# Two sets of three PSUM banks for the jobs of the second attention, and a reordered way into it

## The reference

```python
o_a = swa_sink_attention(q_a, k_a, v_a, swa_sinks[l], rel_bias)     # 16 heads of 64, window 128, bias, sink
q_b = jnp.einsum('bsr,rf->bsf', c_q, w_uq[l]).reshape(B, S, MLA_HEADS, MLA_QK_DIM)
q_nope = q_b[..., :MLA_NOPE_DIM]
q_rope = rope(q_b[..., MLA_NOPE_DIM:], positions)
kv_b = jnp.einsum('bsr,rf->bsf', c_kv, w_ukv[l])...                 # keys k_nope and values v_b of 8 heads
# mla: s = (q_nope k_nope + q_rope k_rope) * scale, causal, softmax, times v_b
mix = jnp.concatenate([o_a, o_b], axis=-1)
x = x + g1 * jnp.einsum('bsm,md->bsd', mix, w_out[l])
```

## Time and profile before

| | |
|---|---|
| median of three executions | 2282.96 us |
| span of the profiled execution | 2283.4 us |
| the slowest execution | 2286.44 us |
| TensorE busy | 2212.5 us, 97% of the span |
| VectorE, ScalarE busy | 1511.5 us, 1011.6 us |
| stretch from the query transposes to step 0 of the projection | 1394.08 to 1456.77 us |

### The profile page before, as it was taken

One profiled execution on the slowest core, in us unless ns is written; L12 is line 12 of the kernel. 1 busy time (PEld: TensorE's weight loads), 2 busy tenths in 40 slices (PEclk: granted clock), 3 DMA queues, 4 the chain that ended last, 5 costly groups with the idle time before them and its releaser, 6 DMA issues.

```text
span 2283.4 us, 29520 instructions
## 1 busy us (share of the span) xinstructions
PE 2212.5 (97%) x11498; PEld 1893.8 (83%) x11498; DVE 1511.5 (66%) x1450; ACT 1011.6 (44%) x1261; POOL 15.1 (1%) x40
## 2 busy tenths in 40 slices
PE   7999999999999999999999898999999999999997
PEld 6888888788888888888878697887888888888886
DVE  6676466777777668767788865557555555655655
ACT  5443273544344344344355544535444444443442
POOL 1000000000000000000000000000000000000000
PEclk9999999999999999999999998999999999999999
DMA  8775407687877877878867353355656656556553
GB/s 323 288 277 177 145 23 281 237 279 279 300 258 288 296 269 256 315 258 287 294 238 283 120 193 111 111 192 155 187 193 179 199 194 195 184 186 202 181 196 122
DMA packets 213107, 499.68 MB, mean 219 GB/s; under 512 B 10068, under 2 KB 12680, under 8 KB 199800
## 3 DMA queue, kind: packets, MB, share of 16 engines
q1 hardware_dynamic: 211528, 491.16, 63.3%
q0 software_dynamic: 1456, 6.72, 0.8%
HBM read 495.68 MB, written 2.17 MB: 218 GB/s over the span
## 4 chain that ended last, share of the span: by engine, by line
PE 60%; issue 36%; DVE 2%; ACT 1%; DMA 1%; SPq 0%; POOL 0%; DVEq 0%; ACTq 0%; POOLq 0%
PE ps L1520 17%; PE ps L1509 9%; PE ps L1511 9%; PE ps L1510 9%; PE ps L1525 9%; PE ps L1692 2%; PE ps L1748 1%; PE ps L1567 1%; PE ps L1620 1%; PE ps L1698 0%; PE ps L1584 0%; PE ps L1634 0%; ACT prob L699 0%; PE ps L1749 0%; PE ps L1746 0%
## 5 line engine op out<-in xcount | busy, mean ns | idle before, releaser
L904 DVE TENSOR_TENSOR lower<-raw,upper 128x1024 fp32r<-128x1024 f32 (+2 forms) x733 | 883.7, 1215 | 522.9 <-ACT upper L496 519.7
L496 ACT ACTIVATE upper<-raw 128x1024 fp32r<-128x1024 f32 (+2 forms) x733 | 769.4, 1055 | 950.3 <-PE ps L1511 530.6
L1520 PE MATMUL ps<-xs,upper 128*128 128x512 f32 x2688 | 675.9, 393 | 5.1 <-DVE h L994 4.3
L1520 PEld LDWEIGHTS ps<-xs,upper 128*128 128x128 f32 x2688 | 484.1, 189 | 93.7 <-issue 6.2
L1509 PE MATMUL ps<-upper,hidden 128*128 128x512 f32 x1024 | 399.2, 390 | 0.0
L1510 PE MATMUL ps<-lower,hidden 128*128 128x512 f32 x1024 | 398.5, 389 | 0.0
L1511 PE MATMUL ps<-upper,hidden 128*128 128x512 f32 x1024 | 398.4, 389 | 0.0
L1525 PEld LDWEIGHTS ps<-xs,lower 128*128 128x128 f32 x2688 | 366.7, 190 | 26.3
L1525 PE MATMUL ps<-xs,lower 128*128 128x256 f32 x2688 | 374.8, 282 | 0.0
L1509 PEld LDWEIGHTS ps<-upper,hidden 128*128 128x128 f32 x1024 | 192.3, 188 | 40.3 <-DVE lower L904 0.9
L1511 PEld LDWEIGHTS ps<-upper,hidden 128*128 128x128 f32 x1024 | 192.2, 188 | 40.0
(11 more groups left out here) (257 smaller groups left out, 1185.8 us busy)
## 6 DMA issues: line engine op xcount, KB each, us to landing
raw<-in_ffn_w_dram SPq DMA_DIRECT2D x128, 1024.0 KB, 6.0
raw<-in_w_ff_dram SPq DMA_DIRECT2D x128, 1024.0 KB, 5.3
modraw<-in_w_mod_dram SPq DMA_DIRECT2D x96, 1024.0 KB, 7.8
raw<-in_nsa_w_in_dram SPq DMA_DIRECT2D x40, 1024.0 KB, 5.2
raw<-in_nsa_w_out_dram SPq DMA_DIRECT2D x16, 1024.0 KB, 7.1
raw<-in_ple_w_gate_dram SPq DMA_DIRECT2D x16, 1024.0 KB, 5.1
raw<-in_w_out_dram SPq DMA_DIRECT2D x16, 1024.0 KB, 5.1
raw<-in_w_in_dram SPq DMA_DIRECT2D x12, 1024.0 KB, 5.2
```

What stands on the lines that cost most here:

```text
L496: nc.scalar.activation(dst, src, ACT.Copy).then_inc(upper_ready, 1)
L904: nc.vector.tensor_tensor(low, src, up, ALU.subtract).then_inc(lower_ready, 1)
L1520: mm(ps[:, 4 * par + f, :], up[:, kk, f * P:(f + 1) * P], both, start=(k == 0), stop=False, skip_group_check=True)
```

## The change

Three edits go together. A late job's scores and its turned probabilities now lie in the same three banks, 0 to 2 for an even job and 3 to 5 for an odd one. The waits change with that: the scores of J10 and of the later ones wait for `probT_ready`, the copy of the job two before, and no longer for `exps`; a turn waits for nothing but its own `prob`; and the projection's step 0 waits for the copy of J12. VectorE rotates the queries ahead of each evacuation of the keys. The rotated queries are turned into banks 6 and 7 (`heads_copied` 3, no `evacuated`), and TensorE waits for the copies of the queries only behind score(J8). ScalarE's order is as it was.

```diff
-        def banks_of(kind):
-            return (3, 0) if kind == "nsa" else (0, 3)
+        def banks_of(n, kind):
+            if kind == "nsa":
+                return 3, 0
+            b = 3 * (n % 2)
+            return b, b
...
+            rotate_queries(0)
             columns_out(0, kn[:, 0:4, :])(0)
-            rotate_queries(0)
+            rotate_queries(1)
             columns_out(0, kn[:, 4:8, :])(0)
-            rotate_queries(1)
...
+                if n > len(NSA_JOBS) + 1:
+
+                    pe.wait_ge(probT_ready, n - 1)
                 for t in range(T):
                     w = P * (t + 1)
-                    if n:
+                    if n and kind == "nsa":
                         pe.wait_ge(exps, 2 * n - 1 + t)
...
-                if n:
+                if n and kind == "nsa":
                     pe.wait_ge(probT_ready, n)
...
-                    if s == 0:
+                    if s == 0 and jobs[last][0] == "nsa":
                         pe.wait_ge(exps, 2 * (base + len(jobs)))
+                    elif s == 0:
+                        pe.wait_ge(probT_ready, base + last)
...
-            pe.wait_ge(evacuated, c.at("groups"))
+            pe.wait_ge(heads_copied, 3)
             pe.wait_ge(roped, T)
...
-                    op = nc.tensor.transpose(ps[:, j // 2, o:o + P],
+                    op = nc.tensor.transpose(ps[:, 6 + j // 2, o:o + P],
...
-            pe.wait_ge(heads_copied, 4)
-            pe.wait_ge(queries_copied, 1)
-            attention(LATE_JOBS, len(NSA_JOBS))
+            pe.wait_ge(evacuated, c.at("groups"))
+
+            def queries_stored():
+                pe.wait_ge(heads_copied, 4)
+                pe.wait_ge(queries_copied, 1)
+
+            attention(LATE_JOBS, len(NSA_JOBS), queries_stored)
```

More of the change, by code:

```diff
@@ L694, in job_exps @@
                         w = P * (t + 1)
-                        sb = banks_of(kind)[0]
+                        sb = banks_of(n, kind)[0]
                         src = ps[:, sb, P * j:P * j + P] if t == 0 else ps[:, sb + 1 + j // 2, S * (j % 2):S * (j % 2) + S]
@@ L705, in job_turned @@
                 act.wait_ge(prob_turned, c.next(prob_turned))
-                tb = banks_of(kind)[1]
+                tb = banks_of(n, kind)[1]
                 if n >= 2:
@@ L873, in _ @@
             heads_out(3, qn[:, 0:4, :].rearrange("p h s -> p (h s)"), 6, 2)
-            heads_out(5, qr[:].rearrange("p h s -> p (h s)"), 0, 2)
+            heads_out(5, qr[:].rearrange("p h s -> p (h s)"), 6, 2)
             attention(LATE_JOBS, len(NSA_JOBS), SCALE.get)
@@ L1211, in attention @@
                     m, par = base + n, (base + n) % 2
-                    sb = banks_of(kind)[0]
+                    sb = banks_of(m, kind)[0]
                     scale = {"nsa": DH ** -0.5, "swa": 1.0, "mla": QK ** -0.5}[kind]
```

## The result

The changed kernel takes 2295.56 us, the median of 4 runs (2295.49 to 2296.01), against 2283.13 us for the kernel before beside it (2282.67 to 2286.44): a ratio of 1.0047, with a 95% interval of 1.0034 to 1.0060. I had forecast slower, 2288.4 us with a range up to 2294.0. The sign is right; the size was under half of what came (5.3 of 12.4 us), and the time lies 1.6 us above the range.

The account below looks back on a forecast made before the run. TensorE was taken to bound the jobs, with waits and half clock ahead of them. Step 0 3.75 us later plus one 1.7 us clock fall made 5.45 us on a 2283.4 us span, 2288.85, so 2288.4 us (range 2284.8 to 2294.0).

Parts of the forecast that it names:

- The way in: Keys to score(J8): rotations moved at no cost, score(J8) starts 4.9 us earlier and ends 8.0 us earlier.
- The cover at the first rotation: Slack left when the first 2.4 us rotation fills VectorE's idle ahead of the key evacuation: 0.35 us.
- The wait for the copy: Ahead of score(J10): TensorE idles 5.0 us until copy(J8), which ScalarE has behind J9's exps.
- The new pace: From J10 to step 0: serial loops, 10.7 us for a windowed job; step 0 comes 3.75 us later.
- The rival in which the lead survives: Chance 0.08: the copy comes as soon as its turn is done, jobs keep the old pace, 2278.6 us.
- The clock: Half clock costs 2.4 us at J10, plus one fall of 1.7 us among four waits ahead of J11 to step 0.
- the rival in which the clock keeps falling: Chance 0.18: three or four falls at the waits behind J10's, +8.9 to +11 us, 2291.8 to 2294 us.
- the last step, from the profile to the median: Forecast span of 2288.85 us, less the 0.4 us by which the profiled span lay above the median: 2288.4 us.

Follow-up runs that it names:

- The copy between the exps: Changed kernel with ScalarE's copy of a job's turned probabilities moved between the next job's t=0 and t=1 exps, for J8 to J12: 2282.09 us.
- the banks alone: Kernel before with only the alternating banks and their waits, the order ahead of score(J8) left as before: 2300.58 us, ratio 1.0072.
- the filled J9 wait: Kernel before with the rotation, bank 6 and 7 and query-copy-wait edits, plus 8 unread bf16 matmuls ahead of J9's t=1 scores: 2279.32 us.
- waits filled: Changed kernel with 19, 10, 9, 8 and 8 unread bf16 matmuls in TensorE's five waits, ahead of J10 to J13 and step 0: 2286.98 us.
- the way in alone: Kernel before with only rotations moved ahead, rotated queries in banks 6 and 7, and query-copy waits behind score(J8); job banks as before: 2278.03 us.

## Why the prediction was right in sign and short in size

**The way in: right.** Transposes with 0.28 us of idle ahead of them, evacuations where they were, score(J8) at 8.77 against 8.89, turn(J8) at 20.39 as forecast. The cover at the first rotation was put at 0.35 us and came out as 0.37, though the rows that it was read from give 0.5 (2.90 us of idle less 2.4); the moved rotation took some 0.1 us longer.

**The wait for the copy: right.** 4.63 us against 5.0, ended by ScalarE's `probT`, which starts behind the exps of J9.

**The new pace: right.** Loops of 10.76 and 10.81 us (score(J12) to score(J13), and on to step 0) against 10.7. The rival in which the lead survives fell on the condition that I gave for it, a loop under 9.5 us. The copy between the exps shows the other side of that point: with the jobs 8.4 to 8.8 us apart the kernel is faster than the one before. One reading was off: J11, J12 and J13 took 8.3, 8.7 and 9.5 us, not 8.3 to 8.8 each; the sum of 26.46 us that the forecast used is right.

The Trainium skill advises to double-buffer for performance ("Trainium Kernel Development and Optimization", Best Practices). Its line speaks of overlapping DMA with compute, and no DMA writes or reads these banks, so it decides nothing here. Two sets of banks in place of two roles cost 10.9 us of stage, since a job's buffer is freed by a copy that its engine does late.

**The clock: right in kind, one fall short.** J10's cost 1.6 us instead of 2.4 (3.1 in another profile), and two more came where I took one. That is 6.05 us on the stage instead of 5.45. No row told which idle brings a fall, and none does now: 2.06 us ahead of step 0 did in all three profiles, 2.47 ahead of J11 in two of three, and 2.38 and 2.02 in none; with the banks alone it was the 2.02 and not the 2.07 or the 2.47. The time lies even above what I gave to the rival in which the clock keeps falling (2291.8 to 2294), yet that rival's (the second in the list, called the third in the text) three or four falls behind J10's did not come: there were two, in another profile one. Its price would have been near the time by luck.

The Trainium skill tells of such a kernel ("TensorE: Matmul & The Clock Gate", A second HAM failure mode: psum-queue depth-cycling), whose idles between groups of matmuls bring the clock down again and again while a matmul at full clock is as fast as ever. The traces agree half way: three falls where I had bet on two, but two of the five waits without one, and the clock is 5.0 of the stage's 87.7 us.

**What failed: the last step, from the profile to the median.** The stage itself was forecast 5.45 us longer and came 6.05 longer. I wrote that "the span has nothing around it and lies 0.4 us above the median". Every profiled execution whose time is known took 1.7 or 1.8 us more than its span (2295.61 against 2293.8 after, 2284.00 against 2282.3 for one of before). So the span of 2288.85 meant a time of 2290.6, and the profile of before took some 2285.2 us, 2 above its median. That is 2.2 of the 7.2 us that I was short.

The second part is what one execution draws. My sum stood on a stage of 81.7 us, where two others have 80.9 and 77.9, and on 2201.7 us outside it, where they have 2205.8 and 2204.4. The changed kernel has 87.7, 87.6 and 87.8 in the stage and 2206.1, 2204.4 and 2204.7 outside. The means differ by 7.6 us in the stage and 1.1 outside. Measured from the means, the change costs 1.5 us more in the stage than from my profile, as the prediction had warned. The mean span after is 2292.8, 3.9 above the forecast; 0.6 of that is the stage, the rest lies outside it, where my profile of before was the quickest of three. The last 1 us is the median of the runs, 2295.5, above the mean of the three profiled executions, 2294.6.

**Over all runs.** Each run carries its span and its mean granted clock. The mean time is 2295.7 us in ten runs of the changed kernel and 2285.0 in 55 of the kernel before, 10.7 apart (the medians differ by some 11.5, since some runs of before reach up to 2291.93). The mean clocks are 0.9877 and 0.9884. Span times clock, the span less what the low clock took, is 2265.7 and 2256.9: 8.8 us of the 10.7 stay with the clock taken out, and 1.8 are clock. Counted in this same way (half of all time at half clock, idle or busy), the stage makes up 7.0 of the 8.8 and 0.6 of the 1.8 (means of three profiles each).

Of the 1.8 us at full clock that are left outside the stage, 1.3 stand in the two places where the kernel with the filled J9 wait lost its gain. TensorE of the changed kernel there:

```profile
1925.84 1.41 PE L1523 MATMUL ps<-xs,upper 128*128 128x512 f32 x5 [0.76 <-issue]
...
2103.51 1.86 PE L1523 MATMUL ps<-xs,upper 128*128 128x512 f32 x7 [0.96 <-issue]
```

The two other profiles of it have 1.38 and 1.54 us there together, the three of before 0.42, 0.40 and 0, and the changed kernel with its waits filled none.

**What stays open.** What makes TensorE idle at these two places, where the change touches nothing. And the clock outside the stage: it took 11.8 us there in the first profile of before and 14.4 in that of after, at places that differ from one execution to the next, and 11.7 with the waits filled. Whether what happens in one stage sets the falls of a later one, no run here tells.

## What to carry to other kernels

Before a buffer is given a second duty, write down what frees it then and where that instruction stands in its engine's order: here a copy of 1.46 us, behind another job's exps, turned jobs 8.3 to 9.5 us apart into jobs 10.8 apart, and ate a gain of 4 us that was already made. Try the parts of a change one by one, since the part that stood by itself (two calls moved into an idle stretch of VectorE) was most of the gain (4.3 of 5.9 us), and the way in alone, at 2278.03 us, beats both kernels. And take the same kernel's profile more than once before trusting a term of a few us: a stage's time less what half clock cost it repeats to 0.2 us (76.0 to 76.2, and 82.8 three times), the stage itself only to 4.

## What the runs showed of the hardware

- Idles of 2.02, 2.06 and 2.47 us on TensorE were followed by 3.4 us at half clock in some places and executions, and not in others. In the kernels whose rotations stand ahead of the evacuations, the idles of 0.28 to 1.32 us at the way in were followed by none.
- Around the same two idles of 3.17 and 1.11 us, the clock of one unchanged kernel was low for 10.24, 6.83 and 3.42 us in three executions.
- Matmuls that nobody reads keep the clock up: 19 of them in bf16, 128x512, took 4.26 us, and the f32 scores behind ran at full clock from the first, where 3.11 to 6.12 us at half clock stood before. They paid 8.5 us (2295.50 to 2286.98, mean clock of all runs 0.9877 to 0.9911) in a kernel with waits of 2 to 4.6 us, and nothing in the one whose wait was 2.06.
- The reported time lies 1.7 to 1.9 us above the span in each execution of this kernel and its variants.
- Two idles of TensorE that the profile puts down to no engine, 180 us apart and far behind the changed stage, took 0 to 1.91 us each, depending on the variant.
